# Shift rows as four column tiles, parameters fetched in parts, and transposed masked matrices of the delta merges by transposes

## The reference, cut to what matters

```python
mod = c_act @ w_ada[l] + b_ada[l]                       # 2048 x 6144
shift, scale, gate = jnp.split(mod, 3, axis=-1)
h = rms_norm(x, norm_g[l]) * (1.0 + scale) + shift
proj = h @ w_in[l]
# state space part of layers 0 and 1
a_bar = jnp.exp(lam * step); b_bar = ((a_bar - 1.0) / lam)[..., None] * b_mat
y = einsum(c_mat, states).real + d_skip * uf
# delta rule of layer 2, per chunk
L = where(strict, einsum(k_beta, k) * decay, 0.0)
t_inv = triangular_solve(eye + L, eye, lower=True, unit_diagonal=True)
u = t_inv @ v_beta;  w = t_inv @ (k_beta * exp(g))
```

## Time and profile before

| | us |
|---|---|
| median of 3 runs | 4494.81 (4494.77 to 4495.7) |
| the profiled execution | 4496.86 |
| its span | 4495.1 |
| PE busy | 4364.2 |
| DVE busy | 1931.7 |
| ACT busy | 815.8 |

### The profile page before, as it was taken

One profiled execution on the slowest core, in us unless ns is written; L12 is line 12 of the kernel. 1 busy time (PEld: TensorE's weight loads), 2 busy tenths in 40 slices (PEclk: granted clock), 3 DMA queues, 4 the chain that ended last, 5 costly groups with the idle time before them and its releaser, 6 DMA issues.

```text
span 4495.1 us, 34105 instructions
## 1 busy us (share of the span) xinstructions
PE 4364.2 (97%) x13146; PEld 2202.3 (49%) x13146; DVE 1931.7 (43%) x3495; ACT 815.8 (18%) x1382; POOL 485.9 (11%) x802
## 2 busy tenths in 40 slices
PE   7899999999999999999999999999999999999999
PEld 3465544444446554444444355555556544444444
DVE  4566536664525563557531543343432234431100
ACT  1122201131011320112300311121211123330000
POOL 0133211111202331111110000000000001100000
PEclk8999999999999999999999999999999999999999
DMA  8433333335442333333443321112121333334322
GB/s 308 173 105 103 118 119 106 119 124 162 151 140 85 96 124 101 129 105 103 152 150 106 100 76 57 57 47 66 57 66 52 108 94 122 112 104 133 105 80 94
DMA packets 368463, 495.16 MB, mean 110 GB/s; under 512 B 44091, under 2 KB 278062, under 8 KB 367790
## 3 DMA queue, kind: packets, MB, share of 16 engines
q1 hardware_dynamic: 289840, 340.16, 23.3%
q0 software_dynamic: 37632, 122.71, 8.6%
q10 hardware_dynamic: 40830, 30.11, 2.1%
HBM read 460.42 MB, written 32.51 MB: 110 GB/s over the span
## 4 chain that ended last, share of the span: by engine, by line
PE 88%; DVE 8%; ACT 1%; ACTq 1%; DMA 1%; issue 1%; POOL 0%; DVEq 0%; SPq 0%
PE bank L108 86%; PE bank L111 2%; DVE tring L117 2%; DVE tring L132 2%; DVE tring L123 2%; ACTq L147 1%; DVE dring L117 1%; DVE dring L120 1%; DVE tring L120 1%; ACT tring L114 1%; DMA yaT<-in_w_ada 0%; DMA SS<-in_w_ada 0%; DVE sring L138 0%; ACT L114 0%; ACT region_b L114 0%
## 5 line engine op out<-in xcount | busy, mean ns | idle before, releaser
L108 PE MATMUL bank<-region_b,wring 128*128 128x512 f32 x4192 | 1872.2, 597 | 6.8 <-ACT region_b L114 6.6
L108 PEld LDWEIGHTS bank<-region_b,wring 128*128 128x128 f32 x4192 | 777.1, 191 | 903.8 <-issue 895.5
L108 PE MATMUL bank<-region_a,wring 128*128 128x512 f32 x2048 | 906.5, 597 | 0.0
L108 PEld LDWEIGHTS bank<-region_a,wring 128*128 128x128 f32 x2048 | 384.6, 191 | 459.3 <-issue 458.0
L147 POOL DMA_DIRECT2D side<-in_w_ada x384 | 208.5, 543 | 1475.8 <-DVE tring L123 920.7
L123 DVE SCALAR_TENSOR_TENSOR tring<-side,cact,tring 128x512 f32<-128x512 f32 x360 | 304.8, 847 | 86.2 <-DMA side<-in_w_ada 50.0
L114 ACT ACT_TABLE_LOAD x196 | 251.5, 1283 | 397.5 <-DVE sring L120 283.7
L108 PE MATMUL bank<-wring,region_b 128*128 128x512 f32 (+1 forms) x640 | 258.2, 559 | 0.0
L108 PE MATMUL bank<-wring,region_a 128*128 128x512 f32 x512 | 226.5, 600 | 6.0 <-ACT region_a L114 6.0
L132 DVE RECIPROCAL tring<-tring 128x512 f32<-128x512 f32 x54 | 180.7, 3347 | 107.6 <-ACT tring L114 107.5
L108 PE MATMUL bank<-yaT,wring 128*128 128x512 f32 x512 | 225.3, 592 | 0.0
(11 more groups left out here) (240 smaller groups left out, 3430.3 us busy)
## 6 DMA issues: line engine op xcount, KB each, us to landing
wring<-in_w_in SPq DMA_DIRECT2D x180, 1024.0 KB, 5.3
side<-in_w_ada POOLq DMA_DIRECT2D x384, 256.0 KB, 3.2
wring<-in_w_out SPq DMA_DIRECT2D x48, 1024.0 KB, 7.0
yaT<-in_w_ada SPq DMA_DIRECT2D x16, 1024.0 KB, 7.3
wring<-in_w_glu SPq DMA_DIRECT2D x16, 1024.0 KB, 8.1
gring<-in_w_ada POOLq DMA_DIRECT2D x64, 256.0 KB, 3.1
tring<-x_saved SPq DMA_DIRECT2D x48, 256.0 KB, 3.0
SS<-in_w_ada SPq DMA_DIRECT2D x8, 1024.0 KB, 8.3
```

The lines of the kernel that those rows point to most:

```text
L108: return self.e.matmul(*a, **k) if self.e else self
```

## The change

Three things, all in the plan and the engines' steps:

1. `first_row` takes as weights not a column of `cact` but 32 columns of a new tile `wide_c` (a `tring` tile, cleared by POOL, into whose first column of each 32 ACT copies the activations), and the four products of a step write four different quarters of the bank's partitions. The four sums stand in four partitions; `first_keep` copies the whole bank and `first_turn` sums over all 128 partitions.
2. `ssm_fetch` is cut in four: small ones with piece 0, C with piece 1, B's real part with piece 2, its imaginary part with piece 3, each with a semaphore of its own; `powers` waits for B.
3. In the merges the products for DM and their subtraction on DVE are gone. `d_join` makes DT alone; a new step `d_dm` transposes DT (four transposes) and ACT copies the result to DM. It has a `yield` of its own, so a pair has 36 yields where it had 32; the ratios of `interleave` become 48/36 and 32/36.

```diff
@@ start, ssm parameters
             temps.take("vrow")
+            temps.take("wide_c")
             do("vec_fetch")
...
-            do("ssm_fetch", l)
+            do("ssm_fetch", l, 0)
             for _ in range(3 if l else 1):
                 yield
+            do("ssm_fetch", l, 1)
             aux.take("prm_turn", l)
...
             do("ssm_params", l, 0)
             yield
+            do("ssm_fetch", l, 2)
             do("ssm_params", l, 1)
             yield
+            do("ssm_fetch", l, 3)
@@ delta
                 aux.take("d_dt", h, n)
+                do("d_join", h, n)
+                aux.give("d_dt", h, n)
+                yield
                 if n < 5:
                     aux.take("d_dm", h, n)
-                do("d_join", h, n)
-                if n < 5:
+                    do("d_dm", h, n)
                     aux.give("d_dm", h, n)
-                aux.give("d_dt", h, n)
-                yield
+                    yield
...
-            interleave(delta_pair(h0 - 2), beside_delta(h0), 48 / 32)
-        interleave(delta_pair(GH - 2), branch_gates(4), 1)
+            interleave(delta_pair(h0 - 2), beside_delta(h0), 48 / 36)
+        interleave(delta_pair(GH - 2), branch_gates(4), 32 / 36)
@@ PE
-                for k in range(k0, k0 + 4):
-                    i = pe.matmul(bank[0:1, :], cact[:, 0, k:k + 1], place[:, k - k0, :], start=k == 0, stop=k == KT - 1)
+                wide = temps.at("wide_c").rearrange("p (k c) -> p k c", k=KT)
+                for n in range(4):
+                    i = pe.matmul(bank[32 * n:32 * n + 32, :], wide[:, k0 + n, :], place[:, n, :], start=k0 == 0, stop=k0 == KT - 4)
...
-                    i = pe.matmul(bank[:, c:c + 1], row[0:1, n * P:(n + 1) * P], ones[0:1, 0:1], start=True, stop=True)
+                    i = pe.matmul(bank[:, c:c + 1], row[:, n * P:(n + 1) * P], ones[:, 0:1], start=True, stop=True)
...
-                pe.wait_ge(*delta_d.of("D", h, n - 1))
+                pe.wait_ge(*(delta_a.of("dm", h, n - 1) if n > 1 else delta_d.of("D", h, 0)))
...
-                if n < 5:
-                    bank = aux.at("d_dm", h, n)
-                    room(aux.clear("d_dm", h, n))
-                    for j in range(TT):
-                        i = pe.matmul(bank[:, J[j]], dq(h, DT)[:, J[j]], dq(h, PM)[:, J[j]], start=True, stop=True)
-                    i.then_inc(*delta_full.up("dm", h, n))
+
+            def d_dm(h, n):
+                bank = aux.at("d_dm", h, n)
+                room(aux.clear("d_dm", h, n))
+                pe.wait_ge(*delta_d.of("D", h, n))
+                for j in range(TT):
+                    i = pe.transpose(bank[:, J[j]], dq(h, DT)[:, J[j]], ident)
+                i.then_inc(*delta_full.up("dm", h, n))
@@ DVE
             def d_join(h, n):
-                if n < 5:
-                    dve.wait_ge(*delta_full.of("dm", h, n))
-                    dve.tensor_tensor(dq(h, DM), dq(h, DM), aux.at("d_dm", h, n)[:, :], SU).then_inc(*d_step.up())
-                    aux.leave(("d_dm", h, n), dve.mine())
@@ ACT
+            def d_dm(h, n):
+                act.wait_ge(*delta_full.of("dm", h, n))
+                act.activation(dq(h, DM), aux.at("d_dm", h, n)[:, :], ACT.Copy).then_inc(*delta_a.up("dm", h, n))
+                aux.leave(("d_dm", h, n), act.mine())
```

More of the change, by code:

```diff
@@ L335, in build @@
         ssm_in = [sem(f"ssm_params_in{l}") for l in range(2)]
+        ssm_c_in, ssm_b_in = [sem(f"ssm_c_in{l}") for l in range(2)], [sem(f"ssm_b_in{l}") for l in range(2)]
         two_in, band_in, band_out = sem("block_two_params_in"), sem("band_in"), sem("band_out")
@@ L1322, in first_row @@
                 pe.wait_ge(*first_landed(SHIFT, j, k0).of(SHIFT, j, k0))
[L1323 to L1324 removed]
+                wide = temps.at("wide_c").rearrange("p (k c) -> p k c", k=KT)
+                for n in range(4):
+                    i = pe.matmul(bank[32 * n:32 * n + 32, :], wide[:, k0 + n, :], place[:, n, :], start=k0 == 0, stop=k0 == KT - 4)
                 i.then_inc(*ada_turned.up("row", j, k0))
+                if j == 3 and k0 == KT - 4:
+                    temps.leave(("wide_c",), pe.mine())
                 aslots.leave(("first", SHIFT, j, k0), pe.mine())
@@ L1388, in c_turn @@
                 room(aux.clear("c_turn", l, i))
-                pe.wait_ge(*ssm_in[l].all())
+                pe.wait_ge(*ssm_c_in[l].all())
                 for t4 in range(4):
@@ L1665, in tensor @@
                          w_turn=w_turn, values=values, band=band_, ba_turn=ba_turn, gate_sums=gate_sums, d_decay=d_decay, d_beta=d_beta, d_kk=d_kk,
-                         d_kq=d_kq, d_kturn=d_kturn, d_vturn=d_vturn, d_first=d_first, d_lo=d_lo, d_join=d_join, d_w=d_w, d_v=d_v,
+                         d_kq=d_kq, d_kturn=d_kturn, d_vturn=d_vturn, d_first=d_first, d_lo=d_lo, d_join=d_join, d_dm=d_dm, d_w=d_w, d_v=d_v,
                          d_step=d_step, w_scores=w_scores, p_turn=p_turn, p_values=p_values, o_turn=o_turn, fence=fence_of(pe))
@@ L2492, in vec_turn @@
                 act.wait_ge(*vec_ready.of("vec"))
-                act.activation(cact[:, :, :].rearrange("p i k -> p (i k)"), vec[:, 0:32], ACT.Silu).then_inc(*att_a.up("silu"))
+                act.activation(cact[:, :, :].rearrange("p i k -> p (i k)"), vec[:, 0:32], ACT.Silu).then_inc(*a_step.up())
+                own()
+                act.wait_ge(*wide_clear.of())
+                act.activation(temps.at("wide_c").rearrange("p (k c) -> p k c", k=KT)[:, :, 0], cact[:, 0, :], ACT.Copy).then_inc(
+                    *att_a.up("silu"))
             def late_fetch():
@@ L2522, in first_keep @@
                 act.wait_ge(*ada_turned.of("row", j, KT - 4))
-                act.activation(temps.at("arow", j)[0:1, :], aux.at("row", j)[0:1, :], ACT.Copy).then_inc(*taken_a.up("row", j))
+                act.activation(temps.at("arow", j), aux.at("row", j)[:, :], ACT.Copy).then_inc(*taken_a.up("row", j))
                 aux.leave(("row", j), act.mine())
@@ L2624, in save_zs, with ssm_fetch @@
                 temps.leave(("zs", l, h0 + j), stored("zs", l, h0 + j).of("zs", l, h0 + j))
-            def ssm_fetch(l):
-                m = lay[l]
+            def ssm_fetch(l, part):
+                m, there = lay[l], (ssm_in, ssm_c_in, ssm_b_in, ssm_b_in)[part][l]
                 def par(dst, src):
-                    act.dma_start(dst, src).then_inc(*ssm_in[l].landing())
+                    act.dma_start(dst, src).then_inc(*there.landing())
                 room(passed("att", l - 1))
+                if part >= 2:
+                    par(m["Bn"][:, part - 2, :, :], bass.AP(d[("ssm_b_re", "ssm_b_im")[part - 2]].tensor, l * 65536, [[16, P], [2048, PAIRS], [1, 16]]))
+                    return
+                if part == 1:
+                    for c, name in enumerate(("ssm_c_re", "ssm_c_im")):
+                        for rep in range(2):
+                            for h in range(2):
+                                room(temps.clear("cn", l, 2 * c + h))
+                                par(temps.at("cn", l, 2 * c + h).rearrange("p (t r n) -> p t r n", t=4, r=2)[:, :, rep, :],
+                                    bass.AP(d[name].tensor, l * 65536 + h * 32768, [[64, P], [8192, 4], [1, 64]]))
+                    return
                 room(temps.clear("prow", l))
@@ L2637, in ssm_fetch @@
                 par(prow[96:128, P:P + 32], bass.AP(d["ssm_d"].tensor, l * HALF, [[32, 32], [1, 32]]))
[L2638 to L2645, removed]
             def sine_cosine(s, c, x, *event):
@@ L2929, in powers @@
                     pool.wait_ge(*ssm_a.of("e_place", l, k - 2))
+                pool.wait_ge(*ssm_b_in[l].all())
                 cmul(W[:, :, 0, 3, :], W[:, :, 1, 3, :], bc(cf[:, 0, qs], 16), bc(cf[:, 1, qs], 16), Bn[:, 0, qs, :], Bn[:, 1, qs, :],
@@ L3007, in band_fetch @@
                         *band_in.landing())
-            steps = dict(ada_fetch=ada_fetch, powers=powers, angles=angles, bc_place=bc_place, lags=lags, rotate=rotate, band=band_,
+            steps = dict(vec_fetch=vec_fetch, ada_fetch=ada_fetch, powers=powers, angles=angles, bc_place=bc_place, lags=lags, rotate=rotate, band=band_,
                          d_qd=d_qd, band_fetch=band_fetch, fence=fence_of(pool))
```

8 lines of the change are left out of this document (6 added, 2 removed).

## The result

The changed kernel takes 4467.57 us (median of 4 runs, 4465.1 to 4468.76), the kernel before in the same comparison 4495.26. The ratio is 0.9938 with a 95% interval of 0.992 to 0.9955: 27.7 us less, where 21.2 were forecast. The profiled execution took 4468.76 us with a span of 4466.9, against 4496.86 and 4495.1, so 28.2 us less span to account for.

The account below looks back on a forecast made before the run. PE, busy 97% of the span, was taken as the bound, with DMA engines and DVE's exponentials bounding parts of the opening. Opening -23.7 and delta +2.5 gave -21.2 us: 4473.6 for the median, range 4461 to 4488.

Parts of the forecast that it names:

- Opening, sum: Opening, rounds 1 to 3 together: 14.4 and 9.3 us saved, 23.7 in all, with bounds 10.8 and 29.
- Price of a row step: Shift rows in the opening: a step's four products fall from 3.6 to 1.6 us, bounds 0.9 and 3.6.
- Rounds 2 and 3: Opening: two cheaper row steps and a cheaper row turn save 4.9 us a round, round 3 paying back about 0.5.
- Round 1: Opening: ACT's issue wait goes, the DMA engines decide, first_out(1) moves from 104.39 to 90.0, 14.4 us saved.
- Late B and positions at 0: After round 3: B's late imaginary part and the positions behind it stay hidden, cost 0, 3 us for the range.
- Moved filler step, 13.7: Delta stage: one filler step of 3.43 us leaves its place ahead of PE's wait in each of four pairs, costing 13.7 us.
- Clock behind the longer waits, +3: Delta stage: after longer waits at d_first the clock is lower for a while, 0.85 us a pair, 3 us in all.
- the forecast's sum: Delta merges: eight DM products replaced by transposes, 0.88 us less in each of 4 merges of 4 pairs, 14.1 us.
- New wait in a merge, 0.6 to 0.7: Delta merges: PE waits 0.6 to 0.7 us for DT ahead of the transposes in three merges a pair, 2 us a pair.
- 1.4 in the last pair: Delta stage, last pair: a merge without a filler step costs 0.8 us more and a chunk step 0.6.
- +2.5: Delta stage as a whole: -14.1 + 13.7 + 3 - 1.5 + 1.4, so 2.5 us longer, the stage gives nothing.
- the forecast's own case: Whole kernel: the time falls between 4466 and 4484 us, given a chance of 0.66.

Follow-up runs that it names:

- early_steps: The changed kernel with the old number of filler steps ahead of d_first in each pair of heads, the rest spread over the later yields; 4446.62 us.
- early_four: The changed kernel with four filler steps ahead of d_first in every pair of heads, the rest spread over the other 34 yields; 4446.66 us.
- delta_alone: The kernel before with only the new delta merges (d_join, d_dm) and their ratios 48/36 and 32/36, old opening; 4492.1 us, ratio 0.9991.
- old_merges_moved: The kernel before, old merges and opening, one filler step less ahead of d_first, in the last pair none ahead of the turns; 4519.56 us.
- the two experiments on the parts: The kernel before with the column tiles alone, 4486.69 us, and the kernel before with the parameters fetched in parts alone, 4485.96 us.
- parts_alone: The kernel before with only ssm_fetch cut in parts, with its semaphores and places; row products and merges stay old; 4485.96 us, ratio 0.9979.
- three_mends: The changed kernel with the exponentials later in rounds 2 and 3, old filler spacing in pairs 1 to 3, four early steps in the last; 4428.93 us.
- tiles_alone: The kernel before with only the column tiles (wide_c, first_row, first_turn, first_keep); B and C in one piece, old merges; 4486.69 us, ratio 0.9981.

## Why the prediction was right, and where its terms were off

**Opening, sum: right.** Forecast -23.7, measured -24.4. In this execution the first product of a row began at 35.15 where it was 37.71 before, since the granted clock from 15 to 24 us was 1.00 in the one and 0.64 in the other. That lead isn't part of the 24.4: `early_steps` and `early_four` have the same opening, begin at 36.77 and 36.22, and have the fourth `first_out` at 161.70 and 161.26, not later than the 162.11 here. With the opening of the kernel before, `delta_alone` and `old_merges_moved` have it at 186.78 and 187.22. Any old against any new gives 24.4 to 26.0.

**Price of a row step: mis-sized.** 1.6 us was taken from two row tiles that share PE; column tiles cost 1.06, near the lower bound of 0.9. Two tiles of 64 rows were the nearest row of the trace, and no measure of four quarters of the columns. The Trainium skill, TensorEngine Tiling (Array Packing), Theoretical Speedup, was nearer: up to 4 times. Start to start the traces have 3.52 us against 1.00, 3.5 times. Key Properties of the same page of the Trainium skill say that a change of mode drains the engine. The filler step behind a row step takes 3.66 us start to start before (89.78 to 93.44) and after (119.16 to 122.82), where one within a run of filler steps takes 3.44 (ten steps from 188.48 to 222.93 before). So the change added no drain; what the 0.2 us are that both kernels pay there isn't shown.

**Rounds 2 and 3: right in kind, off in two terms.** Forecast -4.9 and -4.4, measured -4.0 and -3.9. The chain ahead of the block is unchanged, as the path had it: from `first_out(1)` to the row step it is 22.8 us where it was 22.7. Behind it the two row steps give 5.9 us (5.29 + 3.60 to 1.94 + 1.06), more than the 4.0 forecast. The turns give nothing: the 1.86 us of the earlier trace rows were read behind an 8.10-us wait, at a lower clock, and both turns of a round without that wait took 1.9 before as they do after. And 1.8 us went back to the clock: the filler behind the wait takes 5.66 us where 3.82 is its time. PE has less to do between its waits, and the granted clock of the two rounds fell from 0.89 and 0.92 to 0.77. This last term differs between executions: the same filler steps take 4.44 and 5.25 us in `early_steps`, 5.78 and 4.27 in `early_four`. On the mean of the three executions of either opening the rounds are 4.9 and 4.8 us shorter, so part of the miss of the one trace is chance.

**Round 1: right.** Turns were forecast at 88.1 and stand at 86.01, `first_out(1)` forecast at 90.0 and at 87.89; no issue wait. Most of the 2.1 us go with the earlier start: in `early_four` and `early_steps`, where the first row began 1.1 and 1.6 us later, it is at 88.91 and 89.65. Not as the path had it: PE waited for the third block (2.36 us at 75.07) and not for the fourth, on which the forecast let the round end. That ACT's queue held 9 us, and that tiles gain there only once it is gone, the two experiments on the parts show.

**Late B and positions at 0: right.** In the changed kernel, `parts_alone` and `three_mends` POOL's first read of B stands 0.18 us behind its own memset, and the positions are read 16.6 us or more behind the fourth `first_out`, as before.

**Moved filler step, 13.7: right.** Measured 12.9 for the waits at `d_first` (3.3 + 3.4 + 3.4 + 2.8). But its full cost, with the clock and the waits that it shifts further on, is 20 to 23 us, where 13.7 and the 3 us of clock were forecast.

**Clock behind the longer waits, +3: wrong.** PE's busy time fell by 14.6 us where the products alone are 14.1 by the forecast's sum, so the clock cost nothing net. The step counted the new slow stretches (in the second pair the filler behind `d_first` takes 5.80 us, not 4.67) and not those that went with the waits of 0.90 and 0.85 us (ten filler records behind them took 5.28 us, and 4.46 in the changed kernel).

**New wait in a merge, 0.6 to 0.7: right, a little less.** 0.48 to 0.60, ahead of the second head, in three merges of a pair: 4.6 us in all where 6 were forecast. The waits that went are 5.6 us in the merges and 1.3 ahead of the chunk steps. With 0.25 instead of 1.4 in the last pair, the stage is -3.8 and not +2.5. That is the whole miss of the stage: 3.5 by the clock, 0.8 by the moved step, the rest by the merges' waits. The measured time, 4467.6, lies in the forecast's own case (4466 to 4484), six below its centre.

**What the prediction didn't see** is that the new merges are worth 24 to 27 us, and not 14 to 16. It took the edit and its ratio together. The merges' gain was 10 us or more too small and the cost of the moved step 4 to 6 too small, so the errors partly cancelled, and that the stage came within 6 us is in part luck. Of the 24.1 us at the old spacing 17.4 are PE's busy time (14.1 of it the products, the rest clock) and 6.7 idle time. That the idle time went because DVE has one subtraction a head less ahead of the next LO is argued from the code, not shown by a run.

## What to carry to other kernels

Price an edit and the re-spacing that comes with it apart: run both orders of the filler with both versions of the work, since a null result can be two large numbers that cancel. A filler step is worth its length only ahead of the wait, and a step too many can end a tile whose follow-up stands in front of the awaited work. Before making a producer faster, look for the in-order queue that hands its result on.

## What the runs showed of the hardware

- Four fp32 products with 32-column weights into four quarters of one bank take 1.00 us start to start at full clock, and 3.56 us into one quarter.
- The DMA of 4096 runs of 64 bytes is handed over at once when it is the first such one, and the DMA behind it holds ACT's queue. With 1 MB blocks filling the DMA engines (share 1.11) the first took 0.45 us and the second 12.26; in `tiles_alone` 0.45 and 17.15; in layer 1 of the kernel before (share 0.94) 0.45 and 6.40. Issued alone at 162.58 us in the changed kernel the second took 0.37 us, and the positions' DMA behind it 3.40.
- The granted clock between 15 and 24 us differed between executions of nearly equal work (0.62, 0.64, 0.81, 0.81, 1.00). It moved the first row product between 35.15 and 37.86 us, but not the fourth `first_out`, which stands within 0.9 us in three executions of the new opening.
